# One of four weight sums per seven-product unit moved from VectorE to an accumulating DMA

## The chip, the cores and the metric

The kernel runs on one core of a Trainium2 chip. The metric is the device time of one execution in microseconds (us), the lower the better. Engines are named as the profile names them: PE is TensorE's matmul, PEld its weight load, DVE is VectorE, ACT is ScalarE, POOL is GpSimd, SP is SyncE. A transfer runs on 16 DMA engines, whichever engine issues it.

## What is computed

The program is three transformer blocks on 512 tokens of width 1024, in float32. The change touches the feed-forward parts of the second and third block alone, two in each, so four in all:

```python
def swiglu(x, w13, w2):
    gate, up = jnp.split(x @ w13, 2, axis=-1)
    return (jax.nn.silu(gate) * up) @ w2
...
h = h + 0.5 * rms_norm_2(swiglu(rms_norm_2(h, g[0]), ffn_w13[i, 0], ffn_w2[i, 0]), g[1])
...
h = h + 0.5 * rms_norm_2(swiglu(rms_norm_2(h, g[4]), ffn_w13[i, 1], ffn_w2[i, 1]), g[5])
```

The hidden width is 2816, that is 22 tiles of 128 columns. Every float32 product is made of three matmuls, high x high, low x high and high x low, so every weight needs a high part (`wh`, a rounded copy, made by ACT) and a low part (`wl`, the rest, made by DVE).

## The kernel before

`x @ w13` is worked on tile by tile. One chunk of weights, 128 x 2048 numbers or 1024 KB, holds a gate tile and its value tile over all 1024 inputs. Chunks are loaded by SP into the two halves of `raw` in turn. The first four chunks of a feed-forward part are multiplied plainly; the other 18 are "units" of `sevenths`, in which a 2 x 2 block product is made with seven products in place of eight. There are 4 x 18 = 72 units.

A unit's chunk has four quarters of 128 x 512: `A11` and `A12` (gate), `A21` and `A22` (value). Four sums of them are needed: `S3 = A11 - A21`, `S1 = A21 + A22`, `S2 = A22 - S3` and `S4 = S2 - A12`. They are written over quarters that are no longer needed: `S1` over `A21`. The seven factors `A11`, `S1`, `A22`, `S2`, `A12`, `S4` and `S3` are each split by `high` (ACT) and `low` (DVE) into a ring of eight places. A product is 12 matmuls of 256 columns.

The order on each engine is written out by hand in `emit`. In pass u of its loop:

- PE multiplies A11(u), S1(u), A22(u-1), S2(u), A12(u), S4(u), S3(u). The fourth product of a unit, A22(u-1), waits for `value_made(u-1)` of DVE.
- DVE makes the low part of S3(u), `value_made(u-1)`, the low part of A11(u+1), the sums S3 and S1 of unit u+1 (`add_first_sums`), `second_hidden(u-1)`, the sum S2(u+1), the low parts of S1(u+1) and A22(u), `first_hidden(u-1)`, the low parts of S2(u+1) and A12(u+1), the sum S4(u+1), `first_scaled(u)`, the low part of S4(u+1), `second_made(u)` and `second_scaled(u)`.
- ACT makes the high part of S3(u), `silu(u-1)`, the high part of A11(u+1), `seed(u)`, the high part of S1(u+1), `keep_five(u)`, the high parts of A22(u) and S2(u+1), `keep_u2(u)`, and the high parts of A12(u+1) and S4(u+1).
- SP loads chunk u+2 once the low part of A22(u) is made.
- GpSimd has no work in these loops.

An engine takes its instructions in order, so that one that waits holds back all that stand behind it. The first unit's sums and parts are made ahead, beside the last plain chunk (`first_dve`, `ahead_act`, `ahead_dve`).

Lines of the profile that matter: L2714 is the sum S3, L2715 S1, L2719 S2, L2723 S4; L2707 every low part and L2696 every high part; L2826 `value_made`, L2831 `second_hidden`, L2835 `first_hidden`, L2812 `first_scaled`, L2817 `second_made`, L2821 `second_scaled`; L2762 `seed`, L2766 `keep_five`, L2770 `keep_u2`, L2774 `silu`; L2889 to L2891 the matmuls; L1535 and L1616 transfers that GpSimd issues elsewhere in the program, from SBUF to SBUF.

Of the kernel before, what the change touches and what calls it, by code (L numbers as in the profile page):

```python
# [233 lines left out]
def _build(nc, io, ctx, block):  # L234
# [2283 lines left out]
    EARLY = 8  # L2518
    FIRST, SECOND = slice(0, TH), slice(TH, T)
    w_sums, w_high, w_low, w_made, w_kept, w_gate, w_value = sb_cut, sb_soft_h, sb_soft_l, sb_z, sb_zc, sb_open, sb_keep  # L2520

    class Mixing(Deferred):

# [87 lines left out]
    def sevenths(name, norm, base, halves_, down):  # L2611
# [8 lines left out]
        group = (base + turned[0] - 1) % 2  # L2620
        for s, per in ((w_made, 6), (w_kept, 4), (w_gate, 3), (w_value, 1)):
            s.stage(per, count)
        w_sums.stage(4, count)
        w_high.stage(6, count)
        w_low.stage(6, count)
        last = count - 1
# [2 lines left out]
        MADE, MADE_LAST = ("A11", "S1", "S2", "A12", "S4", "S3"), ("A11", "S1", "S2", "A12", "S3", "S4")  # L2629
        SEED, FIVE, U2, SILU = 1, 2, 3, 4  # L2630
        C11, C12, SCALED = 1, 2, 3
        sum_of = {"S3": 1, "S1": 2, "S2": 3, "S4": 4}

        place_of = {}
        holder = {}
# [15 lines left out]
        def part(buf, u, what):  # L2651
            n = slot(u, what)
            return buf[:, n // 4, n % 4 * QUARTER:(n % 4 + 1) * QUARTER]
# [32 lines left out]
        def high(act, u, what):  # L2686
            at_ = place_of[u, what]
            if what == "A11":
                act.wait_ge(raw_ready[(a + u) % 2], 16 * ((a + u) // 2 + 1))
            if at_ < RING:  # L2690
                act.wait_ge(chunks_used, a + (1 if at_ < 4 else 2))
            else:
                wait_used(act, *name_of[at_ - RING])
            if what in sum_of:
                act.wait_ge(w_sums.sem, w_sums.after(u, sum_of[what]))
            split = nc.scalar.copy(part(wh, u, what), source(u, what))  # L2696
            if what == "A22":
                split.then_inc(hi_ready, 1)
            else:
                split.then_inc(w_high.sem, 1)  # L2700
# [11 lines left out]

        def add_first_sums(dve, u):
            nc.vector.tensor_tensor(source(u, "S3"), source(u, "A11"), source(u, "A21"), ALU.subtract).then_inc(w_sums.sem, 1)  # L2714
            nc.vector.tensor_tensor(source(u, "S1"), source(u, "A21"), source(u, "A22"), ALU.add).then_inc(w_sums.sem, 1)  # L2715

        def add_second_sum(dve, u):
            dve.wait_ge(w_sums.sem, w_sums.after(u, 1))
            nc.vector.tensor_tensor(source(u, "S2"), source(u, "A22"), source(u, "S3"), ALU.subtract).then_inc(w_sums.sem, 1)  # L2719

        def add_fourth_sum(dve, u):
            dve.wait_ge(w_sums.sem, w_sums.after(u, 3))
            nc.vector.tensor_tensor(source(u, "S4"), source(u, "S2"), source(u, "A12"), ALU.subtract).then_inc(w_sums.sem, 1)  # L2723

        def first_act(act):
# [20 lines left out]
        def emit():  # L2746
# [4 lines left out]
            @block.sync  # L2751
            def _(sp):
                for n in range(a, a + count):
                    sp.wait_ge(lo_ready, n + 1)
                    load(sp, n + 2)

            @block.scalar
            def _(act):
                def seed(u):
                    wait_used(act, u, "A11")  # L2760
                    evicted_before(act, u)
                    nc.scalar.copy(bank_b(u), bank_a(u)).then_inc(w_kept.sem, 1)  # L2762

                def keep_five(u):
                    wait_used(act, u, "S1")
                    nc.scalar.copy(five(u), bank_e(u)).then_inc(w_kept.sem, 1)  # L2766

                def keep_u2(u):
                    wait_used(act, u, "S2")
                    nc.scalar.copy(gate_of(u, SECOND), bank_b(u)).then_inc(w_kept.sem, 1)  # L2770

                def silu(u):
                    act.wait_ge(w_gate.sem, w_gate.after(u, SCALED))
                    nc.scalar.activation(gate_of(u, EVERY), gate_of(u, EVERY), ACT.Silu).then_inc(w_kept.sem, 1)  # L2774

                for u in range(count):
                    high(act, u, "S3")
                    if u:
                        silu(u - 1)
                    if u < last:  # L2780
                        high(act, u + 1, "A11")
                    else:
                        halves_.high(act, 0)
                    seed(u)
                    if u < last:
                        high(act, u + 1, "S1")
                    else:
                        halves_.high(act, 1)
                    keep_five(u)
                    high(act, u, "A22")  # L2790
                    if u < last:
                        high(act, u + 1, "S2")
                    else:
                        halves_.high(act, 2)
                        halves_.high(act, 3)
                    keep_u2(u)
                    if u < last:
                        high(act, u + 1, "A12")
                        high(act, u + 1, "S4")
                    else:  # L2800
                        halves_.high(act, 4)
                        wait_used(act, last, "A12")
                        split_hi(act, down, 16 * (down // 2 + 1), down % 2, order[down][2])
                        for t in range(5, EARLY):
                            halves_.high(act, t)
                silu(last)

            @block.vector
            def _(dve):
                def first_scaled(u):  # L2810
                    wait_used(dve, u, "A12")
                    nc.vector.tensor_tensor(gate_of(u, FIRST), bank_a(u), kept[:, FIRST], ALU.mult).then_inc(w_gate.sem, 1)  # L2812

                def second_made(u):
                    wait_used(dve, u, "S4")
                    dve.wait_ge(w_kept.sem, w_kept.after(u, U2))
                    nc.vector.tensor_tensor(gate_of(u, SECOND), gate_of(u, SECOND), bank_e(u), ALU.subtract).then_inc(w_gate.sem, 1)  # L2817

                def second_scaled(u):
                    dve.wait_ge(w_gate.sem, w_gate.after(u, C12))  # L2820
                    nc.vector.tensor_tensor(gate_of(u, SECOND), gate_of(u, SECOND), kept[:, SECOND], ALU.mult).then_inc(w_gate.sem, 1)  # L2821

                def value_made(u):
                    wait_used(dve, u, "S3")
                    dve.wait_ge(w_kept.sem, w_kept.after(u, FIVE))
                    nc.vector.tensor_tensor(five(u), bank_b(u), five(u), ALU.subtract).then_inc(w_value.sem, 1)  # L2826

                def second_hidden(u):
                    dve.wait_ge(w_kept.sem, w_kept.after(u, SILU))
                    dve.wait_ge(w_value.sem, w_value.after(u, 1))  # L2830
                    nc.vector.tensor_tensor(hid[:, WHOLE + u, SECOND], five(u), gate_of(u, SECOND), ALU.mult)  # L2831

                def first_hidden(u):
                    wait_used(dve, u, "A22")
                    nc.vector.tensor_tensor(hid[:, WHOLE + u, FIRST], bank_b(u), gate_of(u, FIRST), ALU.mult).then_inc(psum_read.sem, 1)  # L2835

                for u in range(count):
                    low(dve, u, "S3")
                    if u:
                        value_made(u - 1)  # L2840
                    if u < last:
                        low(dve, u + 1, "A11")
                        add_first_sums(dve, u + 1)
                    else:
                        halves_.low(dve, 0)
                    if u:
                        second_hidden(u - 1)
                    if u < last:
                        add_second_sum(dve, u + 1)
                        low(dve, u + 1, "S1")  # L2850
                    else:
                        halves_.low(dve, 1)
                    low(dve, u, "A22")
                    if u:
                        first_hidden(u - 1)
                    if u < last:
                        low(dve, u + 1, "S2")
                        low(dve, u + 1, "A12")
                        add_fourth_sum(dve, u + 1)
                    else:  # L2860
                        halves_.low(dve, 2)
                        halves_.low(dve, 3)
                    first_scaled(u)
                    if u < last:
                        low(dve, u + 1, "S4")
                    else:
                        halves_.low(dve, 4)
                        value_made(u)
                        split_lo(dve, down, down % 2, order[down][2])
                    second_made(u)  # L2870
                    second_scaled(u)
                halves_.low(dve, 5)
                second_hidden(last)
                first_hidden(last)
                for t in range(6, EARLY):
                    halves_.low(dve, t)
# [1865 lines left out]
```

## Time and profile before

| | |
|---|---|
| median of 3 runs | 3216.35 us (3213.75 to 3219.91) |
| the profiled execution's own time | 3216.84 us |
| its span, first to last instruction | 3215.0 us |
| PE busy | 3147.3 us, 98% |
| DVE busy | 2141.4 us, 67% |
| ACT busy | 1481.6 us, 46% |
| POOL busy | 136.2 us, 4% |
| mean granted TensorE clock | 0.997 |

Busy shares are means over the whole program. The ends of matmuls are modelled: a matmul of 256 columns is shown as 0.28 us long, while the next starts 0.12 us after it, so a short wait between two of them can't be seen in the busy share and is read from the starts. On DVE, too, an instruction is shown longer (0.68 us) than the distance to the next start (0.60 us).

### The profile page before, as it was taken

To read this page: it belongs to the slowest core of one execution; us is meant where nothing else is said; L and a number is where in the kernel's file an instruction comes from. 1 tells how busy PE (TensorE), PEld (TensorE's weight loads), DVE (VectorE), ACT (ScalarE), POOL (GpSimd) and SP (SyncE) were. 2 spreads that over 40 slices of the span, in tenths; PEclk is the share of its full clock that TensorE was granted. 3 is DMA by queue.
4 is the path that set the end of the run, shared out by engine and by line. 5 is a ranking of instruction groups with operands and counts; after the bars stand their busy time and mean duration, and the time that the engine had idled before them with its cause. 6 is when DMAs were issued, how large, how long until landed. Compare 5 with 4: busy or idle time off the path is not lost. (4 is left out here: it accounts for less than half of the span.)

```text
span 3215.0 us, 54209 instructions
## 1 busy us (share of the span) xinstructions
PE 3147.3 (98%) x22914; PEld 2706.6 (84%) x22914; DVE 2141.4 (67%) x3127; ACT 1481.6 (46%) x2289; POOL 136.2 (4%) x134
## 2 busy tenths in 40 slices
PE   9999999999999999999999999999999999999998
PEld 7887787888889988988899887998777787799986
DVE  6546766775389835363888458986666665789737
ACT  3357644443255623432555345554336564455524
POOL 2100000000000001000100011000120000100002
PEclk9999999999999999999999999999999999999999
DMA  5311232222323323223132331332222000123331
GB/s 184 113 53 66 92 105 90 86 101 89 108 79 106 102 99 114 92 79 105 66 106 98 107 104 66 106 106 99 85 81 102 16 4 16 66 96 110 107 102 66
DMA packets 47249, 287.17 MB, mean 89 GB/s; under 512 B 6416, under 2 KB 6688, under 8 KB 21408
## 3 DMA queue, kind: packets, MB, share of 16 engines
q1 hardware_dynamic: 44960, 279.51, 25.6%
q0 software_dynamic: 2048, 4.20, 0.4%
q8 instruction: 182, 2.98, 0.4%
q14 instruction: 59, 0.48, 0.0%
HBM read 277.39 MB, written 2.10 MB: 87 GB/s over the span
## 5 line engine op out<-in xcount | busy, mean ns | idle before, releaser
L345 DVE TENSOR_TENSOR wl<-raw,wh 128x2048 fp32r<-128x2048 f32 (+3 forms) x211 | 425.0, 2014 | 325.2 <-ACT wh L329 324.8
L528 PE MATMUL ps<-xh,wh 128*128 128x512 f32 (+1 forms) x1312 | 519.3, 397 | 20.3 <-DVE wl L345 8.5
L528 PE MATMUL ps<-xl,wh 128*128 128x512 f32 (+1 forms) x1312 | 495.0, 392 | 3.3 <-POOL xl L3535 3.0
L329 ACT CAST wh<-raw 128x2048 fp32r<-128x2048 f32 (+2 forms) x208 | 348.5, 1676 | 277.3 <-PE ps L528 266.2
L528 PE MATMUL ps<-xh,wl 128*128 128x512 f32 (+1 forms) x1312 | 472.5, 393 | 0.3 <-DVE wl L345 0.3
L2696 ACT CAST wh<-raw 128x512 fp32r<-128x512 f32 x432 | 262.6, 620 | 240.4 <-DVE raw L2715 115.9
L528 PE MATMUL ps<-hid_h,wh 128*128 128x512 f32 x880 | 342.9, 390 | 0.9 <-DVE wl L345 0.9
L528 PE MATMUL ps<-hid_l,wh 128*128 128x512 f32 x880 | 342.4, 389 | 0.0
L528 PE MATMUL ps<-hid_h,wl 128*128 128x512 f32 x880 | 342.4, 389 | 0.0
L2707 DVE TENSOR_TENSOR wl<-raw,wh 128x512 fp32r<-128x512 f32 x432 | 297.1, 689 | 66.5 <-ACT wh L2696 65.4
L2889 PE MATMUL ps<-mix_h,wh 128*128 128x256 f32 x1152 | 327.3, 284 | 1.9 <-DVE tmp L2826 1.5
L2890 PE MATMUL ps<-mix_l,wh 128*128 128x256 f32 x1152 | 326.0, 283 | 0.0
L2891 PE MATMUL ps<-mix_h,wl 128*128 128x256 f32 x1152 | 325.9, 283 | 0.0
L528 PEld LDWEIGHTS ps<-xh,wh 128*128 128x128 f32 (+1 forms) x1312 | 246.6, 188 | 87.9 <-issue 28.5
L528 PEld LDWEIGHTS ps<-xl,wh 128*128 128x128 f32 (+1 forms) x1312 | 246.2, 188 | 60.1 <-POOL xl L3535 3.8
L528 PEld LDWEIGHTS ps<-xh,wl 128*128 128x128 f32 (+1 forms) x1312 | 246.0, 188 | 54.6 <-issue 1.0
L2891 PE MATMUL ps<-xh,wl 128*128 128x256 f32 x864 | 244.5, 283 | 0.0
L2890 PE MATMUL ps<-xl,wh 128*128 128x256 f32 x864 | 244.5, 283 | 0.0
L2889 PE MATMUL ps<-xh,wh 128*128 128x256 f32 x864 | 244.5, 283 | 0.0
L2889 PEld LDWEIGHTS ps<-mix_h,wh 128*128 128x128 f32 x1152 | 221.0, 192 | 4.1 <-DVE tmp L2826 2.7
L2890 PEld LDWEIGHTS ps<-mix_l,wh 128*128 128x128 f32 x1152 | 221.1, 192 | 0.0
L2891 PEld LDWEIGHTS ps<-mix_h,wl 128*128 128x128 f32 x1152 | 221.1, 192 | 0.0
(538 smaller groups left out, 5934.7 us busy)
## 6 DMA issues: line engine op xcount, KB each, us to landing
raw<-in_up SPq DMA_DIRECT2D x88, 1024.0 KB, 4.9
raw<-in_down SPq DMA_DIRECT2D x64, 704.0 KB, 4.0
raw<-in_up_c SPq DMA_DIRECT2D x22, 1024.0 KB, 5.0
raw<-in_down_c SPq DMA_DIRECT2D x16, 704.0 KB, 4.0
raw<-in_gates SPq DMA_DIRECT2D x8, 1024.0 KB, 5.0
raw<-in_gv SPq DMA_DIRECT2D x8, 1024.0 KB, 4.9
raw<-in_gu SPq DMA_DIRECT2D x8, 1024.0 KB, 4.9
raw<-in_gout SPq DMA_DIRECT2D x8, 1024.0 KB, 4.8
```

What stands on the lines that cost most here:

```text
L329: nc.scalar.copy(wh[:, slot, 0:w], raw[:, slot, 0:w]).then_inc(hi_ready, 1)
L345: nc.vector.tensor_tensor(wl[:, slot, 0:w], raw[:, slot, 0:w], wh[:, slot, 0:w].bitcast(F32), ALU.subtract).then_inc(lo_ready, 1)
L528: last = nc.tensor.matmul(out, stationary, moving, start=(fresh and q == 0), stop=(t == kt - 1 and half == per - 1 and q == 2), skip_group ...
L2696: split = nc.scalar.copy(part(wh, u, what), source(u, what))
L2707: split = nc.vector.tensor_tensor(part(wl, u, what), source(u, what), part(wh, u, what).bitcast(F32), ALU.subtract)
L2889: nc.tensor.matmul(out, hi_w[:, at_], hi, start=(fresh and j == 0), stop=False, skip_group_check=True)
L2890: nc.tensor.matmul(out, hi_w[:, at_], lo, start=False, stop=False, skip_group_check=True)
L2891: done = nc.tensor.matmul(out, lo_w[:, at_], hi, start=False, stop=(j == KQ - 1), skip_group_check=True)
```

## The change

The sum S1 = A21 + A22 is no longer made by DVE. GpSimd issues a transfer from SBUF to SBUF, one for each unit, which adds A22 (128 x 512 numbers, 256 KB) onto A21 in place. It waits until the sum S3 is made, which is the last to read A21 (`w_sums.after(u, 1)`), and its end is counted by 16 on a semaphore of an earlier stage, `heads_placed`, on which the high part of S1 waits. In ACT's order the high part of S1(u+1) moves behind `keep_five(u)` and the high part of A22(u); in DVE's order the low part of S1(u+1) moves behind the low part of A22(u) and `first_hidden(u-1)`. PE's order stays.

```diff
+    w_joined = Steps(heads_placed, FAR_PLACED)
...
-        w_sums.stage(4, count)
+        w_sums.stage(3, count)
+        w_joined.stage(16, count)
...
-        sum_of = {"S3": 1, "S1": 2, "S2": 3, "S4": 4}
+        sum_of = {"S3": 1, "S2": 2, "S4": 3}
...
+            if what == "S1":
+                act.wait_ge(w_joined.sem, w_joined.after(u, 16))
             split = nc.scalar.copy(part(wh, u, what), source(u, what))
...
         def add_first_sums(dve, u):
             nc.vector.tensor_tensor(source(u, "S3"), source(u, "A11"), source(u, "A21"), ALU.subtract).then_inc(w_sums.sem, 1)
-            nc.vector.tensor_tensor(source(u, "S1"), source(u, "A21"), source(u, "A22"), ALU.add).then_inc(w_sums.sem, 1)
...
+            @block.gpsimd
+            def _(pool):
+                for u in range(count):
+                    pool.wait_ge(w_sums.sem, w_sums.after(u, 1))
+                    pool.dma_start(source(u, "S1"), source(u, "A22"), accum_op=ALU.add).then_inc(w_joined.sem, 16)
...
                     seed(u)
-                    if u < last:
-                        high(act, u + 1, "S1")
-                    else:
+                    if u == last:
                         halves_.high(act, 1)
                     keep_five(u)
                     high(act, u, "A22")
+                    if u < last:
+                        high(act, u + 1, "S1")
...
                     if u < last:
                         add_second_sum(dve, u + 1)
-                        low(dve, u + 1, "S1")
                     else:
                         halves_.low(dve, 1)
                     low(dve, u, "A22")
                     if u:
                         first_hidden(u - 1)
                     if u < last:
+                        low(dve, u + 1, "S1")
                         low(dve, u + 1, "S2")
                         low(dve, u + 1, "A12")
```

On DVE, the stretch from the sum S3 to the low part of A12 in a pass of the loop, before (the low parts are, in order, those of S1, A22, S2 and A12):

```order
L2714 TENSOR_TENSOR raw_50<-raw_50 128x512
L2715 TENSOR_TENSOR raw_50<-raw_50 128x512
L2831 TENSOR_TENSOR hid_4768<-tmp_57 128x256 [waits softplus_and_value_second_made,logits_copied_and_sums_kept]
L2719 TENSOR_TENSOR weight_sum_74_7494<-raw_50 128x512 [waits softplus_cut_and_weight_sums]
L2707 TENSOR_TENSOR wl_52<-raw_50,wh_51 128x512 [waits softplus_and_weight_highs]
L2707 TENSOR_TENSOR wl_52<-raw_50,wh_51 128x512 [waits hi_ready]
L2835 TENSOR_TENSOR hid_4768<-ps,tmp_57 128x256 [waits chunks_used]
L2707 TENSOR_TENSOR wl_52<-weight_sum_74_7494,wh_51 128x512 [waits softplus_and_weight_highs]
L2707 TENSOR_TENSOR wl_52<-raw_50,wh_51 128x512 [waits softplus_and_weight_highs]
```

The same stretch after the change, with the low parts of A22, S1, S2 and A12 in that order:

```order
L2718 TENSOR_TENSOR raw_50<-raw_50 128x512
L2840 TENSOR_TENSOR hid_4768<-tmp_57 128x256 [waits softplus_and_value_second_made,logits_copied_and_sums_kept]
L2722 TENSOR_TENSOR weight_sum_74_7494<-raw_50 128x512 [waits softplus_cut_and_weight_sums]
L2711 TENSOR_TENSOR wl_52<-raw_50,wh_51 128x512 [waits hi_ready]
L2844 TENSOR_TENSOR hid_4768<-ps,tmp_57 128x256 [waits chunks_used]
L2711 TENSOR_TENSOR wl_52<-raw_50,wh_51 128x512 [waits softplus_and_weight_highs]
L2711 TENSOR_TENSOR wl_52<-weight_sum_74_7494,wh_51 128x512 [waits softplus_and_weight_highs]
L2711 TENSOR_TENSOR wl_52<-raw_50,wh_51 128x512 [waits softplus_and_weight_highs]
```

One addition is gone, and the low part of S1 stands behind that of A22 and `first_hidden`.

On ACT, one pass from `silu` on, after the change (the high parts are those of A11, A22, S1, S2, A12, and of S4 and S3 in the last row):

```order
L2783 ACTIVATE tmp_57<-tmp_57 128x512 [waits log_sigmoid_masked_and_gate_halves]
L2700 CAST wh_51<-raw_50 128x512 [waits logits_and_sevenths_made,raw_ready0]
L2771 COPY ps<-ps 128x256 [waits psum_read,logits_and_sevenths_made]
L2775 COPY tmp_57<-ps 128x256 [waits logits_and_sevenths_made]
L2700 CAST wh_51<-raw_50 128x512 [waits logits_and_sevenths_made]
L2700 CAST wh_51<-raw_50 128x512 [waits heads_placed,logits_and_sevenths_made]
L2700 CAST wh_51<-weight_sum_74_7494 128x512 [waits softplus_cut_and_weight_sums,chunks_used]
L2779 COPY tmp_57<-ps 128x256 [waits logits_and_sevenths_made]
L2700 CAST wh_51<-raw_50 128x512 [waits logits_and_sevenths_made]
L2700 CAST wh_51<-raw_50 128x512 [waits softplus_cut_and_weight_sums,logits_and_sevenths_made] x2
```

The high part of S1, which stood between `seed` (L2771) and `keep_five` (L2775), now waits on `heads_placed` two places later, ahead of the high part of S2, `keep_u2` and the high part of A12.

On GpSimd, one feed-forward part has the transfers, 18 in a row, each behind its own wait:

```order
L2764 DMA raw_50<-raw_50 128x512 [waits softplus_cut_and_weight_sums] x18
```

They stand alone in GpSimd's order: its additions for the norms (L931) come before or behind all 18.

## Rows read from the trace of the kernel before

**Rows 1.** The page, part 1: busy time, share of the span and instructions.

```profile
PE 3147.3 (98%) x22914; PEld 2706.6 (84%) x22914; DVE 2141.4 (67%) x3127; ACT 1481.6 (46%) x2289; POOL 136.2 (4%) x134
```

**Rows 2.** Windows from `value_made` of unit 0 to that of unit 16, four parts.

```profile
core 0: us, PE busy (x) PEld busy (x) DVE busy (x) ACT busy (x) POOL busy (x), PEclk, DMA share, GB/s
944.78:1104.58 159.80, 159.57 (x1330) 159.36 (x1329) 144.76 (x273) 87.42 (x177) 0.00 (x0) 1.00 0.31 104
...
sum 641.23, PE 639.33 PEld 637.71 DVE 578.24 ACT 348.77 POOL 0.00; mean PE 159.83 PEld 159.43 DVE 144.56 ACT 87.19 POOL 0.00
```

**Rows 3.** Waits of PE, whole span: us in total, times, longest us.

```profile
PE ps L2889 <- DVE tmp L2826: 1.5, 6, 0.3
```

**Rows 4.** Timeline of DVE, one early pass and its neighbours: start us, us.

```profile
936.61 0.68 DVE L2714 TENSOR_TENSOR raw<-raw 128x512 f32<-128x512 f32 x1
...
944.78 0.42 DVE L2826 TENSOR_TENSOR tmp<-ps,tmp 128x256 f32<-128x256 f32 x1
...
956.00 0.68 DVE L2714 TENSOR_TENSOR raw<-raw 128x512 f32<-128x512 f32 x1
956.60 0.69 DVE L2715 TENSOR_TENSOR raw<-raw 128x512 f32<-128x512 f32 x1
...
959.76 0.68 DVE L2707 TENSOR_TENSOR wl<-weight_sum,wh 128x512 fp32r<-128x512 f32 x1
...
960.96 0.69 DVE L2723 TENSOR_TENSOR raw<-weight_sum,raw 128x512 f32<-128x512 f32 x1
...
962.39 0.69 DVE L2707 TENSOR_TENSOR wl<-raw,wh 128x512 fp32r<-128x512 f32 x1 [0.41 <-ACT wh L2696]
...
964.39 0.42 DVE L2826 TENSOR_TENSOR tmp<-ps,tmp 128x256 f32<-128x256 f32 x1
...
965.74 0.69 DVE L2714 TENSOR_TENSOR raw<-raw 128x512 f32<-128x512 f32 x1
```

**Rows 5.** Timeline of ACT, high parts of A22 and A12 around `keep_u2`.

```profile
948.47 0.62 ACT L2696 CAST wh<-raw 128x512 fp32r<-128x512 f32 x1
...
949.78 0.63 ACT L2696 CAST wh<-raw 128x512 fp32r<-128x512 f32 x1
```

**Rows 6.** Timeline of DVE, sums S3 of two late passes, and the last `value_made`.

```profile
1015.15 0.68 DVE L2714 TENSOR_TENSOR raw<-raw 128x512 f32<-128x512 f32 x1
...
1025.24 0.69 DVE L2714 TENSOR_TENSOR raw<-raw 128x512 f32<-128x512 f32 x1
...
1104.58 0.42 DVE L2826 TENSOR_TENSOR tmp<-ps,tmp 128x256 f32<-128x256 f32 x1
```

**Rows 7.** Timeline of PE, first matmul of product A22 of units 0 and 16.

```profile
945.25 0.38 PE L2889 MATMUL ps<-mix_h,wh 128*128 128x256 f32 x1 [0.23 <-DVE tmp L2826]
...
1106.62 0.28 PE L2889 MATMUL ps<-mix_h,wh 128*128 128x256 f32 x1
```

**Rows 8.** Two lines of GpSimd's transfers: duration of the issue, ns min/median/max.

```profile
L1535 POOL DMA_DIRECT2D qk<-turned_rows x48: 496/496/659, 38.5 to 90.5; - x48
...
L1616 POOL DMA_DIRECT2D va_far<-va x16: 557/557/571, 118.5 to 126.9; - x16
```

**Rows 9.** GpSimd's 64 KB transfers of 38 to 43 us, alone.

```profile
q0 software_dynamic: 208, 0.46, 39.4%
...
DMA to landing us min/median/max: 1.9/1.9/2.0
```

**Rows 10.** The same of 43 to 48 us, with a load of SP.

```profile
raw<-in_ka SPq DMA_DIRECT2D x1, 1024.0 KB, 5.9
...
DMA to landing us min/median/max: 1.8/3.6/5.6
```

**Rows 11.** DMA issues: count, KB each, median us from issue to landing.

```profile
raw<-in_up SPq DMA_DIRECT2D x88, 1024.0 KB, 4.9
...
raw<-in_lora_w SPq DMA_DIRECT2D x1, 256.0 KB, 2.7
```

More of the change, by code:

```diff
@@ L2721, in add_fourth_sum @@
         def add_fourth_sum(dve, u):
-            dve.wait_ge(w_sums.sem, w_sums.after(u, 3))
+            dve.wait_ge(w_sums.sem, w_sums.after(u, 2))
             nc.vector.tensor_tensor(source(u, "S4"), source(u, "S2"), source(u, "A12"), ALU.subtract).then_inc(w_sums.sem, 1)
```

## The prediction, made before the run

> **What bounds the kernel now.** The page comes first: PE is busy for 98% of the span, DVE for 67% [rows 1]. A mean over the program says nothing about the four `sevenths` loops, so the windows are cut there, from `value_made(0)` to `value_made(16)` of each part: 159.8 us in the first, 641.23 us in all four. DVE is busy for 578.24 of these 641.23 us, 90%, and PE for 639.33 [rows 2]. The timelines say who leads. Late in a part, the sums S3 of two passes are 1025.24 - 1015.15 = 10.09 us apart [rows 6], and PE needs 84 matmuls x 0.12 us = 10.08 us for a unit: PE sets the pace. Early in a part they are 965.74 - 956.00 = 9.74 us apart [rows 4]: DVE comes late out of the stage before and catches up 0.34 us in each pass. So DVE is hardly shorter than PE. The waits of PE show what this costs now: `value_made` held up L2889 for 1.5 us in the whole program [rows 3]. Those are starts that one sees; with the ends modelled, the true figure is a few tenths more each time. There are thus only a few us to gain, while a pass of DVE that grows beyond 10.08 us is paid 64 times and more.
>
> **The change, part by part.**
>
> *The addition that goes.* It takes DVE 956.60 - 956.00 = 0.60 us [rows 4] per unit. DVE's own pass falls from 9.74 to 9.14 us if nothing else waits. PE already sets the pace at 10.08, so by itself this is worth nothing but the 1.5 us of waits.
>
> *The new wait.* S3's sum releases GpSimd, the transfer ends D later, ACT then makes the high part of S1, and DVE the low part. Apart from D this is the chain sum, high, low, and S4 shows its length: from the start of its sum to the start of its low part are 962.39 - 960.96 = 1.43 us [rows 4]. So the low part of S1 can start 1.43 + D after the start of S3's sum. In the meantime DVE has `second_hidden`, the sum S2, the low part of A22 and `first_hidden`: with the sum S3 some 2.5 us of work, which cover a D of about 1 us. Then DVE stands still, and all that follows in its order stands with it, up to `value_made(u)`, for which PE waits ahead of A22(u). On ACT the high part of S2, `keep_u2` and the high part of A12 stand behind the same wait.
>
> *The length of a pass.* The next transfer can only be issued when S3's next sum is made, and this sum stands behind the low part of S1 on DVE. So D lies inside a closed loop and no lead that PE has can hide it for long. The loop is:
>
> - from the start of S3's sum to the start of S1's low part: 1.43 + D;
> - S1's low part: 0.60;
> - from the start of S2's low part to the next S3's sum: 965.74 - 959.76 = 5.98 [rows 4];
> - ACT, now late, is late for the low part of A12 too: its high part ends 949.78 + 0.63 - 948.47 = 1.94 us after the start of the high part two ahead of it [rows 5], whose place S1 takes; DVE would be there after about 1.86. With the signal this adds about 0.15.
>
> A pass is 8.16 + D, or 10.08 where that is longer. The break-even is D = 1.92.
>
> *The first pass.* Unit 0's transfer runs while DVE waits for PE anyway, and I cost it at nothing for D up to about 4. In pass 0 the change moves `value_made(0)`: before, it started 944.78 - 936.61 = 8.17 after S3's sum. Now it starts 1.43 + D + 0.60 + 0.15 and then 964.39 - 959.76 = 4.63 [rows 4] after it, so D + 6.81, that is D - 1.36 later.
>
> *The sum.* Before, PE's product A22 went from unit 0 to unit 16 in 1106.62 - 945.25 = 161.37 us [rows 7], while `value_made` went in 159.80 [rows 2, 6]: 1.57 more. I take the same for all four parts: 641.23 + 4 x 1.57 = 647.5 us. After, it is 4 x 16 x (8.16 + D) = 522.2 + 64 D, and four times the first pass, 4 D - 5.4. The change costs 522.2 + 64 D + 4 D - 5.4 - 647.5 = **68 D - 131 us**. The last pass has no transfer and PE's work after it is unchanged.
>
> *D.* The trace has no accumulating transfer. Nearest are GpSimd's transfers of 64 KB from SBUF to SBUF: 1.9 to 2.0 us from issue to landing when alone [rows 9], the issue of 0.50 us included, as I read it (if not, D is 0.5 more). In this stretch of 5 us the queue took 39.4% of 16 engines for 0.46 MB, seven transfers [rows 9]: 0.394 x 5 / 7 = 0.28 us for 64 KB, 1.12 us for 256 KB. As a copy the new transfer would take 2.0 + 0.84 = 2.8 us; the adding one must also read what it adds onto, and if that takes the same again, 2.0 + 2 x 1.12 - 0.28 = 4.0. The issue was 0.50 us for 32 rows and 0.56 us where there were 64 pieces [rows 8]; with 128 rows I add 0.2. So D is 3.0 to 4.2 alone. For a cross-check, a load of 256 KB by SP took 2.7 [rows 11]. I take 3.5.
>
> Can it be covered or lengthened? The load of chunk u+2 (1024 KB, 4.9 us [rows 11]) is issued when the low part of A22 is made, about 1.5 us behind the new transfer in every pass. Most of a short D is over before that data flows, and the end of a long one runs beside it. GpSimd's transfers had a median of 3.6 us and a maximum of 5.6 in a stretch with such a load [rows 10]. That is the upper bound of D; the lower one is the 1.9 of a quarter of the bytes.
>
> The Trainium skill, "DMA: Bandwidth & Descriptors", section "Anatomy of one DMA — SWDGE (gpsimd) path", fits 2.0 us plus the bytes by 436 GB/s: 2.6 us for 256 KB, an estimate by which the sum would be +46. Its "Collectives: The Full Stack", section on the bandwidth ceiling, says that an adding transfer is slower because it needs two source reads; with a second 0.6 us that makes an estimate of 3.2 and +87. The same DMA page advises to issue early and wait late because the fixed part only overlaps with work; the rows agree that the fixed part is most of the 2.0 us, and here little work is left to overlap it.
>
> With D = 3.5 a pass takes 11.66 us, PE stands still for 1.58 us in each, and the cost is 68 x 3.5 - 131 = 107 us. Against the profiled execution's own 3216.84 us this is 3324 us; the median of the runs, 3216.35, lies 0.5 lower, which changes nothing. **3324 us, 3.3% slower.**
>
> **The rivals.**
>
> *Hidden, no loss (5%; faster 2%).* If D were below 1.92 us, DVE's pass would stay under 10.08 and PE would go on setting the pace; the lighter DVE would take away the waits of 1.5 us and the tenths around them, and the time would be 3212 to 3217 us. For it: an addition may be no longer than a copy, and the sum is released early. Against it: a quarter of the bytes already takes 1.9 [rows 9]. A gain above 0.2% has no source in the trace.
>
> *As quick as a copy (15%).* The addition rides along and D is 2.2 to 3.0: 3235 to 3290 us. The 2.7 of SP's load of 256 KB [rows 11] speaks for it; 68 x 2.7 - 131 = +53, 3269 us.
>
> *Two reads, alone (55%).* D from 3.0 to 4.2, 3290 to 3372 us; my forecast.
>
> *It meets the load (23%).* The end of the transfer shares the engines with the 1024 KB load, or the addition itself is slow. D is 4.2 to 5.6 [rows 10], 3372 to 3467 us or somewhat more. Against it: the load is issued 1.5 us behind, and those slow transfers were in part issued behind it.
>
> **How the numbers follow.** What a measurement of this kernel can tell from no change is about 0.2%, 6.4 us, a little more than the spread of the three runs. Within that D must be below about 2.0. The range leaves out D below 2.55 (some 10%: the hidden case and the quickest copies) and above 5.2 (some 10%): 68 x 2.55 - 131 = +42 gives 3259, rounded to 3257; 68 x 5.2 - 131 = +223 gives 3440. Slower 93%, within 0.2% 5%, faster 2%.
>
> **What would show it.** In the profile after: transfers of 256 KB from GpSimd, 72 of them, with a landing of 3 to 4.2 us; S3's sums apart by 8.16 + landing in all passes of a part; DVE and PE with new idle time, DVE ahead of S1's low part, PE ahead of A22 with `value_made` as releaser, some 1.6 us x 64; ACT waiting for a DMA ahead of S1's high part. A pass still 10.08 us long would show the closed loop wrong; a pass that differs from 8.16 + D would show its terms wrong; a right pass length with another D leaves only the size wrong. The forecast also fails if PE's new pauses lower its granted clock, 1.00 in these stretches [rows 2], or if the norms' additions on GpSimd are late behind the transfers.

## The result, and the profile after

The changed kernel takes 3353.47 us in the median of 4 runs (3352.82 to 3354.49), against 3215.05 for the kernel before (4 runs on the same chip). The ratio is 1.0428, with a 95% interval of 1.0414 to 1.0442: 4.3% slower. Forecast were 3324 us, 3.3% slower, in a range of 3257 to 3440. Two executions below stand far outside all others and count in no ratio: one of the kernel before (3447.28 us, at a granted clock of 0.85) and one of the kernel of experiment 4 (9322.71 us, cause unknown).

The page of the changed kernel, parts 1, 5 and 6 (the lines of the program have moved: L2700 is every high part, L2711 every low part, L2718 the sum S3, L2764 the new transfer, L2779 `keep_u2`, L2835 `value_made`, L2898 to L2900 the matmuls):

```profile
PE 3186.4 (95%) x22914; PEld 2720.8 (81%) x22914; DVE 2100.7 (63%) x3055; ACT 1471.5 (44%) x2289; POOL 198.2 (6%) x206
...
L2700 ACT CAST wh<-raw 128x512 fp32r<-128x512 f32 x432 | 259.2, 616 | 412.6 <-DMA raw<-raw 300.4
...
raw<-raw POOLq DMA_DIRECT2D x72, 256.0 KB, 3.5
```

DVE has 72 instructions and 41 us of work fewer than in [rows 1]. ACT stood still for 300 us ahead of its high parts until one of the 72 transfers had landed, which takes 3.5 us in the median from the start of its issue on GpSimd to the last semaphore count; below, this time is called the landing. The windows of the first part, again from `value_made(0)` to `value_made(16)`:

```profile
core 0: us, PE busy (x) PEld busy (x) DVE busy (x) ACT busy (x) POOL busy (x), PEclk, DMA share, GB/s
947.34:1136.50 189.16, 169.36 (x1345) 162.87 (x1344) 135.65 (x257) 84.77 (x177) 13.73 (x16) 1.00 0.37 110
```

Sixteen passes take 189.16 us, 11.82 each, where [rows 2] has 159.80. The clock granted to PE is 1.00 as before, so the time is not lost there. The waits of PE in the changed kernel (us in total, times, longest us), to be read beside [rows 3]:

```profile
PE ps L2898 <- ACT tmp L2779: 73.2, 62, 7.3
PE ps L2898 <- DVE tmp L2835: 26.2, 60, 0.4
```

The timeline of DVE in one pass shows the loop, with every instruction from one sum S3 to the low part of S2, and the next sum S3:

```profile
995.90 0.68 DVE L2718 TENSOR_TENSOR raw<-raw 128x512 f32<-128x512 f32 x1
996.50 0.42 DVE L2840 TENSOR_TENSOR hid<-tmp 128x256 f32<-128x256 f32 x1
996.83 0.69 DVE L2722 TENSOR_TENSOR weight_sum<-raw 128x512 f32<-128x512 f32 x1
997.43 0.69 DVE L2711 TENSOR_TENSOR wl<-raw,wh 128x512 fp32r<-128x512 f32 x1
998.04 0.42 DVE L2844 TENSOR_TENSOR hid<-ps,tmp 128x256 f32<-128x256 f32 x1
1001.09 0.69 DVE L2711 TENSOR_TENSOR wl<-raw,wh 128x512 fp32r<-128x512 f32 x1 [2.64 <-ACT wh L2700]
1001.70 0.69 DVE L2711 TENSOR_TENSOR wl<-weight_sum,wh 128x512 fp32r<-128x512 f32 x1
...
1007.74 0.69 DVE L2718 TENSOR_TENSOR raw<-raw 128x512 f32<-128x512 f32 x1
```

In the same pass, the timelines of GpSimd and of ACT:

```profile
996.88 0.85 POOL L2764 DMA_DIRECT2D raw<-raw  x1 [10.93 <-DVE raw L2718]
```

```profile
1000.44 0.62 ACT L2700 CAST wh<-raw 128x512 fp32r<-128x512 f32 x1 [4.10 <-DMA raw<-raw]
1000.97 0.61 ACT L2700 CAST wh<-weight_sum 128x512 fp32r<-128x512 f32 x1
1001.49 0.36 ACT L2779 COPY tmp<-ps 128x256 f32<-128x256 f32 x1
```

The chain is: the sum S3 ends at 996.58, GpSimd issues 0.30 us later, the high part starts at 1000.44 and the low part at 1001.09. DVE stands still for 2.64 us ahead of it. From the start of S3's sum to the start of S1's low part it is 5.19 us; the forecast had 1.43 + D. So the whole D, from the sum's end to ACT's release, is 5.19 - 1.43 = 3.76 us: 0.30 until the issue and 3.5 of landing. Of these, 3.76 - 2.64 = 1.12 us are covered by other work of DVE. From the low part of S1 to that of S2 it is 0.61, from there to the next sum 6.04, and the pass is 11.84.

### The profile page after: what moved, and what is told of

Its sections match the earlier page's. It is cut to its first block and busy times, and to the rows that moved or that the text cites. A ratio compares the mean times of both kernels' runs of the same rounds, so it can differ in the third digit from the quotient of the medians.

```text
span 3352.7 us, 54209 instructions
## 1 busy us (share of the span) xinstructions
PE 3186.4 (95%) x22914; PEld 2720.8 (81%) x22914; DVE 2100.7 (63%) x3055; ACT 1471.5 (44%) x2289; POOL 198.2 (6%) x206
## 5 line engine op out<-in xcount | busy, mean ns | idle before, releaser
L2711 DVE TENSOR_TENSOR wl<-raw,wh 128x512 fp32r<-128x512 f32 x432 | 297.7, 690 | 257.5 <-ACT wh L2700 256.4
L2700 ACT CAST wh<-raw 128x512 fp32r<-128x512 f32 x432 | 259.2, 616 | 412.6 <-DMA raw<-raw 300.4
L2898 PE MATMUL ps<-mix_h,wh 128*128 128x256 f32 x1152 | 341.7, 297 | 99.5 <-ACT tmp L2779 73.2
L2900 PE MATMUL ps<-mix_h,wl 128*128 128x256 f32 x1152 | 327.7, 284 | 0.0
L2898 PEld LDWEIGHTS ps<-mix_h,wh 128*128 128x128 f32 x1152 | 221.8, 193 | 125.9 <-ACT tmp L2779 86.7
L2898 PE MATMUL ps<-xh,wh 128*128 128x256 f32 x864 | 247.1, 286 | 0.0
L2900 PE MATMUL ps<-xh,wl 128*128 128x256 f32 x864 | 246.5, 285 | 0.0
L2900 PEld LDWEIGHTS ps<-mix_h,wl 128*128 128x128 f32 x1152 | 222.5, 193 | 0.0
```

Of the source, the lines that this page charges most:

```text
L2711: split = nc.vector.tensor_tensor(part(wl, u, what), source(u, what), part(wh, u, what).bitcast(F32), ALU.subtract)
L2898: nc.tensor.matmul(out, hi_w[:, at_], hi, start=(fresh and j == 0), stop=False, skip_group_check=True)
L2900: done = nc.tensor.matmul(out, lo_w[:, at_], hi, start=False, stop=(j == KQ - 1), skip_group_check=True)
```

## The experiments

Eight kernels were run. Each is named with its median, the median of the kernel before on the same chip, and the ratio with its 95% interval. A pass is timed from one sum S3 to the next; there are 64 such passes in the four parts, the first one of each part left out.

**1. Is it the closed loop on DVE, or ACT's queue that holds PE?** PE's longest waits in the changed kernel name `keep_u2` on ACT, which stands behind the transfer, and not `value_made` as forecast. So `keep_u2` is moved ahead of S1's high part (this and the edits below are against the changed kernel, if nothing else is said):

```diff
                     high(act, u, "A22")
+                    keep_u2(u)
                     if u < last:
                         high(act, u + 1, "S1")
...
-                    keep_u2(u)
```

> The changed kernel with keep_u2(u) moved ahead of the high part of S1(u+1) on ACT, so that it no longer stands behind the transfer. In the changed kernel PE waits 73 us for keep_u2 and 26 us for value_made. Theory A, closed loop on DVE (sum S3, transfer, high and low part of S1, and all of DVE's pass up to the next S3): the waits for keep_u2 go, PE arrives earlier at product A22 and waits there for value_made instead; a pass stays 11.7 to 11.85 us, the time 3344 to 3354 us (the high part of A12 comes 0.1 us earlier). Theory B, PE is held by ACT, whose queue stands behind the transfer: the 73 us come back, a pass is about 10.8 us, the time about 3280 us.

3351.39 us against 3215.60, ratio 1.0414 (1.0398 to 1.0430). The waits of PE in this kernel, and its timeline where a pass's A22 begins (`value_made` is L2834 here):

```profile
PE ps L2897 <- DVE tmp L2834: 97.1, 61, 3.2
```

```profile
1007.24 0.39 PE L2897 MATMUL ps<-mix_h,wh 128*128 128x256 f32 x1 [1.42 <-DVE tmp L2834]
```

The 73 us of waits for `keep_u2` turned into as many more for `value_made`, the median pass went from 11.83 to 11.74, and the time stayed within 2.1 us. Theory A stands. The chain of waits of the changed kernel named who came last at a place, not what made the pass long: two waits in one loop share one loss.

**2. Does the move of S1's parts cost anything?** The kernel before, with the addition on DVE and only the places changed:

```diff
                     seed(u)
-                    if u < last:
-                        high(act, u + 1, "S1")
-                    else:
+                    if u == last:
                         halves_.high(act, 1)
                     keep_five(u)
                     high(act, u, "A22")
+                    if u < last:
+                        high(act, u + 1, "S1")
...
-                        low(dve, u + 1, "S1")
...
                     if u < last:
+                        low(dve, u + 1, "S1")
                         low(dve, u + 1, "S2")
```

> The kernel before, with the addition S1 still on DVE, and only the high and low part of S1 two places later as in the changed kernel. Theory A: the move costs nothing by itself, passes of 9.7 us while DVE catches up and 10.08 us later, 3212 to 3219 us. Rival: the later place of S1's parts takes a lead away from PE or holds the high part of S2 back, and a part of the 137 us is its: above 3225 us.

3210.63 us against 3215.60, ratio 0.9983 (0.9974 to 0.9993, 10 runs). It costs nothing and even gains 5 us, a little more than I expected. The sums S3 of this kernel on DVE, two early passes and the first at PE's pace:

```profile
954.41 0.68 DVE L2714 TENSOR_TENSOR raw<-raw 128x512 f32<-128x512 f32 x1
...
964.01 0.68 DVE L2714 TENSOR_TENSOR raw<-raw 128x512 f32<-128x512 f32 x1
...
973.62 0.68 DVE L2714 TENSOR_TENSOR raw<-raw 128x512 f32<-128x512 f32 x1
...
983.69 0.68 DVE L2714 TENSOR_TENSOR raw<-raw 128x512 f32<-128x512 f32 x1
```

A pass bound by DVE is 9.60 us, not 9.74 as in [rows 4], and PE's waits in the loops, 1.5 us in [rows 3], are no longer among its longest. This is the fastest of all kernels here.

**3. Does the place of S1's parts set how much of the transfer is covered?** The transfer stays, the parts go back:

```diff
                     seed(u)
-                    if u == last:
+                    if u < last:
+                        high(act, u + 1, "S1")
+                    else:
                         halves_.high(act, 1)
                     keep_five(u)
                     high(act, u, "A22")
-                    if u < last:
-                        high(act, u + 1, "S1")
...
                         add_second_sum(dve, u + 1)
+                        low(dve, u + 1, "S1")
```

> The changed kernel with the high and low part of S1 at their old places, ahead of keep_five and the high part of A22 on ACT and of the low part of A22 and first_hidden on DVE. Theory A: 0.93 us of DVE's work (0.60 and 0.33) leaves the cover of the transfer, a pass is about 12.7 us instead of 11.82. The load of the next chunk is now issued when the transfer has landed, so that the few transfers of over 5 us go. 64 x 0.9 = 58 us more and up to 20 us less: 3385 to 3412 us. Theory B, DVE's order plays no part: 3350 us as the changed kernel.

3411.20 us against 3215.60, ratio 1.0604 (1.0589 to 1.0618). Transfers on line L2764, and two sums S3 on DVE:

```profile
DMA to landing us min/median/max: 3.2/3.2/4.4
```

```profile
1014.12 0.68 DVE L2718 TENSOR_TENSOR raw<-raw 128x512 f32<-128x512 f32 x1
...
1026.75 0.69 DVE L2718 TENSOR_TENSOR raw<-raw 128x512 f32<-128x512 f32 x1
```

A pass is 12.6 us, in the median of the 64 passes 12.67, so 0.84 more than in the changed kernel: 0.93 less cover, a landing that is 0.3 shorter because the load now starts behind it, and 0.2 that DVE waits between the low parts of S1 and A22, whose high parts ACT makes with `keep_five` between them. The two places were worth 58 us, as expected.

**4. Is the loss gone once the cover is long enough?** S1's high part goes behind that of A12, its low part behind `first_scaled`:

```diff
-        SPLIT = ("A11", "S1", "S2", "A12", "S4", "S3")
+        SPLIT = ("A11", "S2", "A12", "S1", "S4", "S3")
...
                         high(act, u + 1, "A12")
+                        high(act, u + 1, "S1")
                         high(act, u + 1, "S4")
...
                     first_scaled(u)
                     if u < last:
+                        low(dve, u + 1, "S1")
                         low(dve, u + 1, "S4")
```

> The changed kernel with the high part of S1(u+1) behind that of A12(u+1) on ACT, and its low part behind first_scaled(u) on DVE, ahead of the low part of S4; the transfer as it is. From the start of S3's sum DVE then has about 4.6 us of work ahead of the low part of S1, which can start after 5.2 us. Theory A: DVE's pass is 9.3 to 9.5 us, PE sets the pace at 10.08 us, and the loss is gone: 3212 to 3222 us, with the transfer still 3.5 us long. Rival, the transfer costs by its bandwidth or by holding up loads, SBUF or GpSimd: above 3260 us whatever the place.

3223.34 us against 3215.60, ratio 1.0020 (1.0011 to 1.0029). Of the 138 us of loss, 130 are gone, with the same 72 transfers of 3.4 us. DVE's sums S3, early:

```profile
945.61 0.69 DVE L2718 TENSOR_TENSOR raw<-raw 128x512 f32<-128x512 f32 x1
...
954.73 0.69 DVE L2718 TENSOR_TENSOR raw<-raw 128x512 f32<-128x512 f32 x1
```

A pass of DVE alone is 9.12 us, near the 9.14 that the forecast gave a DVE without the addition, and PE sets the pace at 10.08 from the fourth pass on. So the rival is out: with the same transfers and the same loads, only the work ahead of the wait was changed. The 3223.34 us lie 1 us above what I expected. What is left sits in two passes of 14.07 and 15.94 us, together 9.9 us above the median. They are the passes of the same two transfers, the 48th and the 65th, that are the longest in the changed kernel. In the first of them, GpSimd's timeline, the landing, and what the DMA queues moved from 2109 to 2113 us (packets, MB, share of the 16 engines):

```profile
2108.76 0.87 POOL L2764 DMA_DIRECT2D raw<-raw  x1 [10.58 <-DVE weight_sum L2722]
```

```profile
DMA to landing us min/median/max: 7.1/7.1/7.1
```

```profile
q1 hardware_dynamic: 95, 0.78, 74.0%
```

The sum S3 before it started at 2106.41, so the transfer was issued 1.66 us after the sum's end, not 0.30 as all the others but one. SP's load was issued at 2108.90, and for 4 us its queue was the only one that moved anything: the first packet of the transfer started 5.0 us after its issue, where in an ordinary pass it is 1.4. So the transfer landed after 7.1 us.

**5. Addition or copy.** `accum_op=ALU.add` is left out, so that S1 is A22 and not the sum.

> The changed kernel with a plain copy of A22 over A21 in place of the addition: same bytes written, same rows, same issuing engine; it leaves the addition of S1 out, so that S1 is A22. Landing of the adding transfer: 3.2 us without a load beside it, 3.5 with. If the addition itself costs time (second read of each row), the copy lands at 2.6 to 2.9 us and the time falls by 68 us per us, to 3295 to 3315 us. If the addition is free and the length comes from the 128 rows and the fixed part, it lands at 3.2 to 3.5 and the time stays at 3335 to 3354 us.

3265.20 us against 3216.12, ratio 1.0150 (1.0135 to 1.0165). Transfers on L2764 and two sums S3:

```profile
L2764 POOL DMA_DIRECT2D raw<-raw x72: 536/536/571, 927.1 to 3048.3; - x72
...
DMA to landing us min/median/max: 2.2/2.3/6.0
```

```profile
970.08 0.68 DVE L2718 TENSOR_TENSOR raw<-raw 128x512 f32<-128x512 f32 x1
...
980.70 0.68 DVE L2718 TENSOR_TENSOR raw<-raw 128x512 f32<-128x512 f32 x1
```

The copy is quicker than either of my cases, and so the time is 30 us below the lower one: it lands after 2.3 us, against 3.2 for the addition alone (experiment 3) and 3.5 beside the load. The issue on GpSimd falls from 0.86 to 0.54 us. The flow of bytes, in 40 slices of 0.1 us, of the copy in this kernel (981 to 985 us, issued at 981.68; the 164 near the start is a packet of instructions, and from the 30th slice on it is the load) and of the addition in the kernel of experiment 3 (1015 to 1019 us, issued at 1015.10):

```profile
GB/s 0 0 0 164 0 0 0 0 0 0 0 0 0 0 0 0 0 123 410 451 328 492 451 328 41 0 0 0 0 410 328 246 0 0 164 0 246 246 246 164
```

```profile
GB/s 0 0 0 0 0 0 0 0 0 0 0 0 0 0 0 184 164 246 205 184 246 225 164 225 205 205 225 143 1 0 0 0 0 0 0 0 0 0 0 0
```

The copy flows for about 0.75 us at some 400 GB/s, the addition for 1.3 us at some 200, and it starts 0.4 us later after its issue. The queue of GpSimd's transfers in the same two windows (packets, MB, share), first the copy and then the addition:

```profile
q0 software_dynamic: 80, 0.26, 16.1%
```

```profile
q0 software_dynamic: 144, 0.26, 36.2%
```

The copy goes out as 64 packets of 4 KB, the addition as 128 of 2 KB, and each with 16 of 4 bytes.

**6. Less data.** The transfer adds only 128 of 512 columns; for the other 384 the addition is left out.

> The changed kernel whose transfer adds only the first 128 of 512 columns, 64 KB in 128 rows of 512 B; it leaves the addition out for the other 384 columns. Closed loop: a pass is 8.1 to 8.2 us plus the 0.3 us from the sum to the issue plus the landing, so that passes and landing move one for one. The issue stays 0.85 us (128 rows), the landing falls to 2.3 to 2.6 us as less data flows, passes to 10.6 to 11.0 us, the time to 3260 to 3290 us. If the time didn't hang on the length of the transfer, it would stay at 3352 us.

3279.27 us against 3216.12, ratio 1.0194 (1.0179 to 1.0209). Landing 2.3 us in the median, passes of 979.65 - 968.98 = 10.67 us:

```profile
968.98 0.69 DVE L2718 TENSOR_TENSOR raw<-raw 128x512 f32<-128x512 f32 x1
...
979.65 0.69 DVE L2718 TENSOR_TENSOR raw<-raw 128x512 f32<-128x512 f32 x1
```

Landing, pass and time came as expected: the time hangs on the length of the transfer, whether it is shortened by a copy or by moving less.

**7. The load kept away from the transfer.**

```diff
                     sp.wait_ge(lo_ready, n + 1)
+                    if n + 1 < a + count:
+                        sp.wait_ge(w_joined.sem, w_joined.after(n + 1 - a, 16))
                     load(sp, n + 2)
```

> The changed kernel in which SP issues the load of the next chunk only when the adding transfer of the pass has landed. Theory: in the changed kernel the tail of each transfer runs beside the head of the load (3.5 us instead of 3.2), and a few are caught whole (4.7 to 8.4 us). Both go: landing 3.2 us in nearly all passes, passes of 11.5 us, the longest under 13.5, 3352 - 0.3 x 64 - 15 = about 3318 us (3312 to 3328), the load still in time. Rival: the 3.5 us and the long ones have another cause (GpSimd, SBUF): 3345 to 3355 us; or the load is now late for the next chunk's A11: over 3352 us.

3331.43 us against 3216.12, ratio 1.0357 (1.0341 to 1.0372). The transfers, now on L2766:

```profile
DMA to landing us min/median/max: 3.2/3.2/5.3
```

The 3.2 came as expected and passes fell to 11.58. The long passes didn't go: seven are still over 0.5 us above the median, 13.8 us together, against 18.3 in the changed kernel, with landings of up to 5.3 us while no load ran. Only in the two longest did the load have a part: 7.0 us fell to 3.2 and 8.4 to 5.2. I was wrong by the time of those passes, and the 3331.43 us lie 3 us above my range.

The trace shows what the others have in common. Six transfers landed late here, after 4.8 to 5.3 us: the 27th, 30th, 33rd, 53rd, 65th and 71st. The queues from 1766 to 1772 us, with the 33rd, issued at 1766.45, and no load's data under way:

```profile
q0 software_dynamic: 144, 0.26, 24.5%
q8 instruction: 1, 0.02, 2.0%
```

In each of the six a packet of 16 KB of instructions started 1.5 to 2.7 us after the issue, which is while the transfer's own data flowed (1.43 to 2.87 us in an ordinary one), and in none of the other 66 did one start in that time. In experiment 3, too, the only two that landed above 4 us, the 3rd and the 33rd, are the only two with such a packet. In experiment 5 such packets started 1.9 to 2.0 us behind the issue of the 27th, 30th, 33rd, 53rd and 71st copy, when their data was all but through, and these landed after the usual 2.3 us. No run moved a packet by itself, so that it delays the addition is what fits the records, not what an experiment has shown.

**8. GpSimd adds by itself.**

```diff
-                    pool.dma_start(source(u, "S1"), source(u, "A22"), accum_op=ALU.add).then_inc(w_joined.sem, 16)
+                    nc.gpsimd.tensor_tensor(source(u, "S1"), source(u, "A21"), source(u, "A22"), ALU.add).then_inc(w_joined.sem, 1)
```

> The changed kernel in which GpSimd makes the sum S1 itself, by an addition of two tiles of 128 x 512 in SBUF, in place of the transfer; places of the parts as in the changed kernel. GpSimd's additions of this size took 1.28 to 1.74 us in the kernel before. Closed loop with D of about 1.9 us: a pass is 10.0 to 10.1, PE sets the pace, 3210 to 3222 us. Rival: DVE and GpSimd hold each other up while both read two tiles, the addition takes 2 us or more or DVE's own instructions grow, a pass is up to 10.9 us: up to 3270 us.

3220.11 us against 3216.12, ratio 1.0009 (0.9999 to 1.0018). The timeline of GpSimd and of DVE in one pass:

```profile
1008.07 1.41 POOL L2764 TENSOR_TENSOR raw<-raw 128x512 f32<-128x512 f32 x1 [8.70 <-DVE raw L2718]
```

```profile
1008.24 1.78 DVE L2722 TENSOR_TENSOR weight_sum<-raw 128x512 f32<-128x512 f32 x1
```

The addition takes 1.4 us in place of the 3.76 of D, but the sum S2 that DVE starts beside it takes 1.78 us instead of 0.69. The Trainium skill, "SBUF — State Buffer", section "Who interferes with whom", says that a DVE instruction with two SBUF inputs contends with a GpSimd instruction that reads SBUF; this row agrees. So 0.60 us taken from DVE comes back as 1.1, and a pass is 10.10 us in the median (63 of the 64 are 9.95 to 10.11), no shorter than PE's 10.08: no gain either. As DVE's own pass was 9.74 before [rows 4], DVE is slower here than it was.

## Why the prediction was right, and where it was short

*The bound.* PE's pace of 10.08 and DVE's pass of 9.74 were read rightly. Experiment 4 shows DVE at 9.12 without the addition, and that this is worth nothing, since PE sets the pace.

*The closed loop.* It was the main step, and it was right. Four kernels with the same places have these medians of 72 landings and 64 passes:

| kernel | landing, us | pass, us | pass - landing |
|---|---|---|---|
| copy (5) | 2.26 | 10.61 | 8.35 |
| a quarter added (6) | 2.32 | 10.68 | 8.36 |
| load behind (7) | 3.23 | 11.58 | 8.35 |
| as changed | 3.48 | 11.83 | 8.35 |

The pass follows the landing one for one. The forecast had 8.16 and left out that 0.30 us pass between the sum's end and GpSimd's issue; the terms from the low part of S1 on were 0.1 too large (6.65 measured, 6.73 forecast). By experiments 3 and 4 only the work that DVE has ahead of S1's low part decides how much is hidden, and by experiment 1 ACT's queue does not.

*Where PE waits.* Here a step failed: I said PE would stand still ahead of A22 for `value_made`. It did so for 26 us, and for 73 ahead of S3 for `keep_u2`. I had written that `keep_u2` stands behind the same wait and drew no conclusion from it. Experiment 1 shows that this changes the place and not the sum; there PE stands still ahead of A22 alone, and the 1.42 us shown are 1.42 + 0.28 - 0.12 = 1.58 us by the starts of the matmuls, as forecast.

*D.* The landing of 3.5 us is the value taken, but its parts were not: as a copy 2.3 (forecast 2.8), 0.9 more for adding (1.2 forecast for the second read if it took as long again, and 0.2 for the rows), and 0.3 of meeting the load (forecast as a rival). Experiment 5 shows the first two, experiments 3 and 7 the third. What the forecast lacked for the whole D was the 0.30 us ahead of the issue. That the landing came to the 3.5 taken is in part luck: 3.5 was chosen within a range for a transfer alone, which lands after 3.2, and the other 0.3 came from the load, which the forecast had left to a rival.

*The size.* Measured are 3352.7 - 3215.0 = 137.7 us of span, forecast 107. The 64 passes between the sums S3 take 775.3 us instead of 638.8, 136.5 more. Of the 30 missing, 64 x (11.83 - 11.66) = 11 are the issue that I left out, less the terms that were too large. 1 us is the first pass of the four parts, where `value_made(0)` moved by 2.40 us and not by 2.14. 18.3 are seven passes of over 0.5 us above the median, which I had not foreseen: I had the load beside the transfer as a rival for all passes and not as a few. The longest of them, in the changed kernel's timeline of DVE, takes 18.29 us:

```profile
3044.66 0.69 DVE L2718 TENSOR_TENSOR raw<-raw 128x512 f32<-128x512 f32 x1
...
3062.95 0.69 DVE L2718 TENSOR_TENSOR raw<-raw 128x512 f32<-128x512 f32 x1
```

Its transfer was issued 1.85 us after the sum's end, at 3047.20, behind a load issued at 3046.92, and took 8.4 us; its first packet started 4.6 us after the issue.

*The rivals.* Hidden: out, as D is 3.76. As quick as a copy: out for the addition, and right for the copy itself. The load: right for two transfers, and worth 0.3 us for the others.

What stays open is why the 48th and the 65th transfer are issued 1.4 and 1.6 us late (in the changed kernel and in those of experiments 1, 3, 4, 6 and 7 alike; of the copies of experiment 5 only the 65th, by 3.1 us). In the changed kernel this late issue puts the transfer beside the load's, and so costs more than itself. The other five long passes are those of the 27th, 30th, 33rd, 53rd and 71st transfer, with a packet of instructions 1.6 to 3.3 us behind the issue, as in experiment 7; that the packet is the cause was not tested by a run.

## What to carry to other kernels

A wait in an in-order queue costs the latency of what is waited for, less the work that stands between its release and its use; where the release itself stands behind the last use on that queue, this is paid in every pass, and no lead of the other engines hides it. Count that cover in us before work leaves an engine that another engine outlasts anyway: here 0.6 us went onto a path of 3.8 us with 1.1 us of it covered, and 2.1 us more of work ahead of the use turned a loss of 138 us into one of 8. Try the change of places by itself: here it was the only part that gained, if only 0.2%.

## What the runs showed of the hardware that was not expected

- An adding transfer of 256 KB from SBUF to SBUF takes 3.2 us from issue to landing alone, the same transfer as a copy 2.3 us; GpSimd's issue takes 0.86 us with the addition and 0.54 without, for the same 128 rows.
- A quarter of the columns, 64 KB in 128 rows, still takes 0.86 us to issue and 2.3 to land: the issue of the addition did not depend on the bytes. How far it goes by rows no run shows; the copies took 0.50 us with 32 rows [rows 8] and 0.54 with 128.
- The copy of 256 KB goes out as 64 packets of 4 KB, the addition as 128 of 2 KB.
- An adding transfer issued within 0.3 us of a load of 1024 KB starts its data 4.6 to 5.0 us after the issue and lands after 7.0 to 8.8 us (experiments 1 and 4 and the changed kernel); issued 1.3 us ahead of the load it lands after 3.5.
- From the end of the sum on DVE to the issue on GpSimd 0.30 us pass; from the landing to ACT's start 0.08.
- A 1.4 us addition on GpSimd made a DVE addition beside it 1.78 us long instead of 0.69.
